# Four down groups by seven products in two of three parts of a decoder layer, with gate and up pairs on five banks

## The reference, cut to what matters

```python
x = x + jnp.concatenate([h_m, y_c], axis=-1) @ w_out      # after the mixer: h_m, y_c from a @ w_in
f = rmsnorm(x, g_ffn)
x = x + (jax.nn.silu(f @ w_gate) * (f @ w_up)) @ w_down   # (S,1024) @ (1024,2816) twice, (S,2816) @ (2816,1024)
e = rmsnorm(pe @ w_ple, g_ple)
x = x + jax.nn.sigmoid(x @ w_pg) * e
```

## Time and profile before

| | us |
|---|---|
| median of 3 runs | 2586.02 |
| lowest, highest | 2583.62, 2588.82 |
| profiled execution | 2582.85 |
| its span, first to last instruction | 2580.8 |

### The profile page before, as it was taken

How to read it: one execution, slowest core, us unless ns; L and a number is a source line. 1 busy time by engine, 2 the same in 40 slices (tenths; PEclk the granted TensorE clock), 3 DMA queues, 4 the chain that set the end, 5 groups by cost and what they waited for, 6 DMA issues and landing times.

```text
span 2580.8 us, 40956 instructions
## 1 busy us (share of the span) xinstructions
PE 2456.6 (95%) x15757; PEld 2395.0 (93%) x15757; DVE 1493.5 (58%) x2327; ACT 909.7 (35%) x1694; POOL 1010.7 (39%) x785
## 2 busy tenths in 40 slices
PE   7899888999999999999999999998999999999998
PEld 6888778999999989999999999998899999999997
DVE  7768987665555684477643333468357763333355
ACT  5344443343334443334312112355234422221133
POOL 5656755576666342122322122333222332322233
PEclk9999999999999999999999999999999999999999
DMA  7556644575666756575555544575667555565544
GB/s 230 211 181 239 219 152 173 202 264 215 212 228 218 229 159 205 182 259 162 180 163 196 203 138 165 180 231 181 192 188 255 169 196 158 189 219 167 175 133 149
DMA packets 285043, 501.00 MB, mean 194 GB/s; under 512 B 18427, under 2 KB 182612, under 8 KB 284342
## 3 DMA queue, kind: packets, MB, share of 16 engines
q1 hardware_dynamic: 212182, 273.59, 31.5%
q10 hardware_dynamic: 72672, 224.82, 26.6%
HBM read 374.70 MB, written 123.65 MB: 193 GB/s over the span
## 4 chain that ended last, share of the span: by engine, by line
PE 72%; DVE 7%; DMA 4%; issue 2%; ACT 1%; POOL 1%; DVEq 0%; SPq 0%; ACTq 0%; POOLq 0%
PE bank L612 23%; PE bank L614 22%; PE bank L613 22%; DMA wring<-weight_parts 2%; DVE qlo L1802 1%; POOL wring L2709 1%; DMA weight_parts<-wring 1%; DMA xs<-x_prompt 1%; DVE ess L2427 1%; PE bank L749 1%; PE bank L738 1%; PE bank L804 0%; PE bank L727 0%; DVE wraw L1792 0%; DVE hid L2444 0%
## 5 line engine op out<-in xcount | busy, mean ns | idle before, releaser
L2709 POOL TENSOR_TENSOR wring<-wraw,wring 128x512 fp32r<-128x512 f32 x525 | 766.6, 1468 | 1219.5 <-ACT wring L1288 1217.3
L612 PE MATMUL bank<-qhi,wring 128*128 128x352 f32 (+1 forms) x3540 | 1154.6, 326 | 69.9 <-DVE u L1913 13.9
L614 PE MATMUL bank<-qhi,wring 128*128 128x352 f32 (+1 forms) x3540 | 1137.2, 321 | 0.0
L613 PE MATMUL bank<-qlo,wring 128*128 128x352 f32 (+1 forms) x3540 | 1135.6, 321 | 0.0
L612 PEld LDWEIGHTS bank<-qhi,wring 128*128 128x128 f32 x3540 | 671.4, 190 | 95.7 <-issue 78.8
L613 PEld LDWEIGHTS bank<-qlo,wring 128*128 128x128 f32 x3540 | 670.7, 189 | 0.0
L614 PEld LDWEIGHTS bank<-qhi,wring 128*128 128x128 f32 x3540 | 668.8, 189 | 0.0
L1288 ACT ACTIVATE wring<-wraw 128x512 fp32r<-128x512 f32 x531 | 331.6, 629 | 712.1 <-PE bank L614 544.0
L612 PE MATMUL bank<-hid,wring 128*128 128x352 f32 (+1 forms) x1056 | 339.8, 322 | 12.2 <-DVE wide L2510 7.2
L614 PE MATMUL bank<-hid,wring 128*128 128x352 f32 (+1 forms) x1056 | 338.5, 321 | 0.0
L613 PE MATMUL bank<-hid,wring 128*128 128x352 f32 (+1 forms) x1056 | 337.7, 320 | 0.0
(11 more groups left out here) (322 smaller groups left out, 2405.2 us busy)
## 6 DMA issues: line engine op xcount, KB each, us to landing
wring<-weight_parts ACTq DMA_DIRECT2D x418, 512.0 KB, 4.5
weight_parts<-wring SPq DMA_DIRECT2D x201, 512.0 KB, 3.9
wraw<-w_down SPq DMA_DIRECT2D x33, 1024.0 KB, 7.2
wraw<-w_in SPq DMA_DIRECT2D x14, 1024.0 KB, 7.2
wraw<-w_gate SPq DMA_DIRECT2D x11, 1024.0 KB, 6.0
wraw<-w_up SPq DMA_DIRECT2D x11, 1024.0 KB, 6.2
wraw<-w_in SPq DMA_DIRECT2D x44, 256.0 KB, 5.1
wraw<-w_gate SPq DMA_DIRECT2D x44, 256.0 KB, 3.8
```

The costliest lines, as they stand in the source:

```text
L612: nc.tensor.matmul(o, hi, mh, start=begins, stop=False, skip_group_check=True)
L613: nc.tensor.matmul(o, hi, ml, start=False, stop=False, skip_group_check=True)
L614: return nc.tensor.matmul(o, lo, mh, start=False, stop=ends, skip_group_check=True)
L2709: nc.gpsimd.tensor_tensor(wlo[e % RING][:, :].rearrange(v, k=k), w.src, whi[e % RING][:, :].rearrange(v, k=k), ALU.subtract).then_inc(lo_d ...
```

## The change

It does five things.
1. In parts 1 and 2 the down groups g = 1 to 4 are done by seven products for each 512 columns of output (`down_by_sevens`): an entry holds a quarter of 2 k x 2 column blocks, and each product runs for two blocks m, on banks `DOWN_BANKS`. The hidden parts of the two pairs are the quarters B11, B12 and B2 of the activations; their differences T1 to T4 are made in `draw` by VectorE, and split into `dhi` and `dlo` by ScalarE and VectorE during the gate pair ahead of the down.
2. Part 0 makes and stores the sums of those down weights from its raw down weights: 32 more spares (`spares_of`, `DOWN_SPARES`), twelve in each group with pg's four: one after the down's last entry, three in the up pair, four in the next gate pair, four in the next up pair. A raw down weight keeps its buffer until its sums are made.
3. All gate and up pairs but up 1, gate 2 and up 2 have five banks and so the order `FIRST_PRODUCTS`.
4. Parts 1 and 2 have two raw buffers (the space of the other two holds `dlo` and `draw`); there SP loads raw r in step r. In part 0 from r = 26 on, SP first stores the parts of raw r-1 and then loads raw r+1.
5. Loads of pg's weights for the spares are issued at other steps, and the DMA scratch is 256 in place of 512.

```diff
-SPARE_PAIRS = {3: 0, 5: 4, 7: 8, 9: 12}
+DOWN_SEVEN = (1, 2, 3, 4)
+DOWN_SPARES = (3,), (1, 3, 5), (0, 2, 4, 6), (0, 2, 4, 6)
+PG_SPARE_LOADS = {24: 0, 32: 1, 38: 2, 44: 3}
+DOWN_PRODUCTS = PRODUCTS
+DOWN_BANKS = ((6, 7, 3, 4), (5, 2, 0, 1))
...
+        b = r % 2 if q else r % RAW_RING
...
-        if st == "gate":
-            return (0, 1, 2, 6, 7) if i == 0 else (0, 1, 2)
-        if st == "up":
-            return (3, 4, 5)
+        if st in ("gate", "up"):
+            own = (0, 1, 2) if st == "gate" else (3, 4, 5)
+            return own if (st, i) in (("up", 1), ("gate", 2), ("up", 2)) else own + (6, 7)
...
+    def spares_of(q, w, p):
+        g = (p - 1) // 2
+        if q or g not in DOWN_SEVEN:
+            return {}
+        of = [("down", g, 0)] * 4 + [("down", g, 1)] * 4 + [("pg", g - 1)] * 4
+        turn = {"down": 0, "up": 1 if p % 2 else 3, "gate": 2}[w]
+        before = sum(len(js) for js in DOWN_SPARES[:turn])
+        if w == "gate" and p % 2:
+            return {}
+        return {j: of[before + k] for k, j in enumerate(DOWN_SPARES[turn])}
...
+            def down_by_sevens(q, g):                                  # TensorE
+                begins = ("P1", "P6", "P5", "P7", "P4")
+                for a in range(2):
+                    for name in DOWN_PRODUCTS:
+                        e, op = n_entry[0], OPERAND_OF[name]
...
+                        entry_ready(e)
+                        if not a:
+                            pe.wait_ge(h_lo, down_operand_low(q.n, g, op))
+                        for m in range(2):
+                            first, second, third, fourth = DOWN_BANKS[m]
+                            bk = {"P1": first, "P2": first, "P5": second, "P3": second, "P6": third, "P4": third, "P7": fourth}[name]
+                            take(bk)
+                            for k in range(2):
+                                last = three(bank[bk][:, 0:q.N], hi[:, k, m, :], lo[:, k, m, :], dhi[:, op, k, 0:q.N],
+                                             down_low(op)[:, k, 0:q.N], name in begins and k == 0, k == 1)
...
-                    raw()                                              # SP
+                    now = q.n * RAWS + r
+                    if not q.n and r > 25:
+                        keep_parts((now - 1,))
+                    raws_to(now if q.n else r + 2 if r < 26 else r + 1)
...
+            def difference_high(q, p, name):                           # ScalarE
+                act.wait_ge(h_lo, HID_LOW[(q.n, p - 1, (0, "T1")) if name == "T1" else (q.n, p, (0, name))])
+                nc.scalar.activation(dhi[:, DIFFERENCES[name], :, 0:q.N], difference(name)[:, :, 0:q.N], ACT.Copy).then_inc(h_hi, 1)
...
-                    if s == 3 and p:
-                        act.wait_ge(h_lo, HIDDEN[(q.n, p - 1, 0, None)])
+                    if s in (1, 2) and p % 2 and seven_pair(q.n, p - 1):
+                        for name in (("T1", "T2"), ("T3", "T4"))[s - 1]:
+                            difference_high(q, p - 1, name)
+                    if p and s == (3 if p == 2 else 1):
+                        act.wait_ge(h_lo, HID_LOW[(q.n, p - 1, last_hidden(q.n, p - 1, 0))])
...
+            def hidden_parts(q, p, c):                                 # VectorE
+                if p % 2:
+                    nc.vector.tensor_tensor(dlo_first[:, c, 0:q.N], u[:, 0], dhi[:, 0, c, 0:q.N], sub).then_inc(h_lo, 1)
+                    nc.vector.tensor_tensor(t_1, u[:, 1], u[:, 0], sub).then_inc(h_lo, 1)
+                    return
+                nc.vector.tensor_tensor(dlo_rest[:, 0:2, c, 0:q.N], u, dhi[:, 1:3, c, 0:q.N], sub).then_inc(h_lo, 1)
+                nc.vector.tensor_tensor(t_2, u[:, 1], t_1, sub).then_inc(h_lo, 1)
+                nc.vector.tensor_tensor(t_3, u[:, 1], t_3, sub).then_inc(h_lo, 1)
+                nc.vector.tensor_tensor(t_4, u[:, 0], t_2, sub).then_inc(h_lo, 1)
...
+                    if s in (1, 2, 5, 6) and p % 2 and seven_pair(q.n, p - 1):
+                        difference_low(q, p - 1, {1: "T1", 2: "T2", 5: "T3", 6: "T4"}[s])
```

More of the change, by code:

```diff
@@ L1071, in raw, with raws_to @@
                     return
-                if r >= RAW_RING:
-                    sp.wait_ge(lo_done, raw_end[r - RAW_RING])
+                if raw_before[r] is not None:
+                    sp.wait_ge(lo_done, raw_end[raw_before[r]])
                 for where, src in raws[r]:
-                    sp.dma_start(wraw[r % RAW_RING][:, where].rearrange("p (k n) -> p k n", k=src.shape[1]), src)\
-                        .then_inc(landed[r % RAW_RING], 16)
+                    sp.dma_start(wraw[raw_buffer[r]][:, where].rearrange("p (k n) -> p k n", k=src.shape[1]), src)\
+                        .then_inc(landed[raw_buffer[r]], 16)
+            def raws_to(r):
+                while n_raw[0] <= r:
+                    raw()
             def keep_parts(which, names=None):
@@ L1239, in _ @@
                         keep_parts(pairs_[now - 1], lambda w: w.prepared >= raw_end[pairs_[now - 1][0]])
-                    if now and now not in pairs_ and now - 1 not in pairs_:
+                    if now and now not in pairs_ and now - 1 not in pairs_ and (q.n or r < 26):
                         keep_parts((now - 1,))
@@ L1283, in one_ahead @@
                 if w.first:
-                    act.wait_ge(landed[w.raw % RAW_RING], raw_landed[w.raw])
+                    act.wait_ge(landed[raw_buffer[w.raw]], raw_landed[w.raw])
                 if w.total:
@@ L1566, in e_square, with down_by_sevens @@
                 nc.scalar.activation(esq[:, :, 0:q.T], q.U[:, 2 * x:2 * x + 2, 0:q.T], ACT.Square).then_inc(e_sq, 1)
+            def down_by_sevens(q, g):
+                n = PAIR_NO[(q.n, "up", 2 * g + 1)]
+                for a in range(2):
+                    for name in DOWN_PRODUCTS:
+                        ahead()
+                        if name != "P1":
+                            continue
+                        for m in range(2):
+                            bk, key = DOWN_BANKS[m][0], (q.n, "down", g, 2 * a + m)
+                            act.wait_ge(*written[key + ("P1",)])
+                            act.wait_ge(*drained[(q.n, "down", g, m, "P7") if a else PAIR_KEYS[n - 2 + m] + ("P3",)])
+                            nc.scalar.activation(t1[(n + m) % 2][:, 0:q.N], bank[bk][:, 0:q.N], ACT.Copy).then_inc(free[bk], 1)
+                            t_used[n + m] = key + ("P7",)
             def late_silu(q, p):
@@ L1745, in link, with own @@
                 dve.wait_ge(dve_own, n_own[0])
+            def own(ins):
+                n_own[0] += 1
+                ins.then_inc(dve_own, 1)
+                return dve_own, n_own[0]
             def wait_buffer(t):
@@ L2858, in _ @@
                     if down_before(p) is not None:
-                        for k in range(8 if down_before(p) else 4):
+                        for k in range(14 if down_seven(q.n, down_before(p)) else 8 if down_before(p) else 4):
                             ahead()
```

242 lines of the change are left out of this document (180 added, 62 removed).

## The result

The changed kernel takes 2634.43 us (median; 2631.27 to 2638.08), the kernel before 2586.28 beside it: ratio 1.0184, 95% interval 1.017 to 1.0198. It is slower by 48.2 us. The forecast was 2593, in a range that ends at 2611: the sign came out, the size did not.

A forecast was written before the change was run, and what follows sets the result against it. TensorE was taken as the bound, busy 2456.6 of 2580.8 us. Terms -30.2 + 4 + 1 - 7.5 + 40 = +7.3 us gave 2590.2, and 3.2 more for the median gave 2593 us, range 2568 to 2611.

The forecast's parts named there:

- Products saved: Down groups of parts 1 and 2: 168 matmuls for 192 at an unchanged price each, -30.2 us.
- VectorE and ScalarE in parts 1 and 2: Gate pairs ahead of downs: ScalarE's wait delays a stored-weight load, 0.5 us in each of eight groups, +4 us.
- Five banks: Gate and up pairs: own banks for P7 and P4 remove part 0's 6.0 us bank waits; -7.5 us with weight waits.
- DMA and two raw buffers: Parts 1 and 2: more loads, raw weights issued only one pair ahead; late raws cost +1 us, bounds 0 and +3.
- The sums of part 0: Part 0's four groups: twelve sums where four were made, 10 us a group, +40 us; bounds +14.4 and +63.
- (a): Part 0's three pairs: ScalarE's cast waits for P5's ring slot, delaying the copy of t; 1.2 us each, 3.6 a group.
- (b): Part 0's gate and second up: cast waits for a store landing behind a raw load; 3.2 us twice, 6.4 a group.
- (c): Part 0's three pairs: GpSimd's 32 entries take 49.3 us, barely fitting beside the products; adds nothing more.
- The first two: Rivals on part 0's sums: stores land early, 2568 us (chance 0.27); stores land 1 us sooner, no change, 2585 us (0.16).
- the third: Rival: VectorE or the load behind ScalarE's wait bounds gate pairs before downs, parts 1 and 2; 2609 us, chance 0.09.
- The fourth: Rival: GpSimd and VectorE run serially in part 0's three pairs, 18 us a group, 2625 us; chance 0.06.
- The rule that stood with it: Two-input VectorE SBUF instructions and GpSimd SBUF reads share a port pair; the loser fully blocks, so all durations add up.

The follow-up runs named there:

- e11: Changed kernel with ScalarE's copies of differences spread over three steps and its wait moved behind a stored-weight load in parts 1 and 2: 2627.43 us.
- e5: Kernel before plus the five banks alone, P2 third: 2581.97 us, ratio 0.9980.
- e3: Changed kernel with both orders altered in part 0: SP stores ahead of the raw load, ScalarE's copy to t ahead of the casts: 2618.60 us.
- e9: e3 with VectorE's sums of the down weights cut to 32 of 512 columns, GpSimd's splits and transfers whole: 2599.13 us.
- e1: Changed kernel with only SP's order altered: in part 0 the first three part stores go ahead of the next raw load: 2620.91 us.
- e13: Changed kernel with both part 0 orders mended, ScalarE's wait moved, sums placed 2, 2, 4, 2, 2 and earlier raw loads: 2582.34 us.
- e15: Changed kernel with only e13's places of the sums and earlier raw loads, old orders kept: 2622.32 us.
- e10: e3 with GpSimd's splits of the down weights' sums cut to 32 of 512 columns, VectorE's sums and transfers whole: 2595.08 us.
- e16: e13 with one of the gate pair's two sums moved to the second up pair (2, 2, 4, 1, 3): 2609.89 us.
- e17: e13 with no sums in the gate pair and four in the second up pair (2, 2, 4, 0, 4): 2604.71 us.
- e2: Changed kernel with only ScalarE's order altered: in part 0 pairs with down sums, P1 is copied to t before the casts: 2621.41 us.

## Why the prediction was wrong, step by step

**Products saved, -30.2.** Right: four times 3.6 us in part 1 and 3.5 in part 2 are -28.4.

**VectorE and ScalarE in parts 1 and 2, +4.** The mechanism was right to the instruction: the load behind ScalarE's wait was expected at 6.5 us into the pair and went out at 6.6. It landed 5.8 us later (1561.2), not 4.5, near the case that the forecast priced at 1.2 us a group, and TensorE waited 0.85 us there. The price was some 5 to 8 us for the 4 forecast: e11, without that wait, is 7.9 us faster, and TensorE's waits on stored weights are 5.2 us less in its trace.

**Five banks, -7.5.** Right in its mechanism: the 6.0 us on the bank are gone. The gain is 4.3 us by e5, whose interval of 2.3 to 8.0 does not exclude 7.5; the waits that came instead, 2.3 us, stood in no term. **DMA and two raw buffers, +1**, was not measured by itself.

**The sums of part 0, +40.** This is the step that failed. The sums cost 73.2 us, 33 more than the forecast had, of an error of 41 in all (48.2 us measured against 7.3). With -28.4, +7.9 and -4.3 they add up to +48.4. Of the 33, some 14 are waits (54.0 us for the 40 of the forecast) and some 17 slow matmuls, of which the forecast has none. Term by term, for a group:
(a) was right: 1.2 us in the first up pair, as predicted.
(b) had the right chain and too small a price. A wait of 4.4 us (1.2 and 3.2) was forecast for the gate and for the second up pair; 5.8 and 5.6 were found, up to 8.2 in part 0. Two things make the difference: three casts in a row stand ahead of the copy of t (the forecast had two), and the first of them already waits 4.96 us for a landing. The kernel before has such a place in its trace: five stores issued from 614 to 621 us beside two raw loads took a median of 10.7 us, and ScalarE waited 6.29 us for a landing (until 627.32).
What was missing is the clock. Behind the two long waits of the group shown the granted clock was 0.50 for 19 and 14 matmuls, 4.6 us. The forecast took every matmul at 160 ns.
(c) "adds nothing" held for the changed kernel, whose waits name GpSimd nowhere in this stretch, but only because the copy of t was later still. e3 shows that with t in time GpSimd's line is the gate pair's bound at almost the same height (23.4 us for 22.4), which is why mending the orders gave 20 us and not 72.

The profile that was to come named the right wait, TensorE idle until the copy of t, with ScalarE waiting on stores; the group of part 0 was to take 90 to 100 us and took 102.60.

**The rivals.** The first two did not come about. Of the third, the load did land in about the 6 us that it asked for, but at a cost of some 8 us in all, not 20. The fourth, GpSimd and VectorE one after the other, had 18 us a group and 2625 us, nearest to the result, and yet not its cause: all 54.0 us of waiting were on ScalarE. It comes nearest to the bound that lies beneath, GpSimd's line in the gate pair. The rule that stood with it, from the Trainium skill (SBUF — State Buffer, "Who interferes with whom"), fits e3's gate pair better than the rows before: 1.73 us for a split and up to 1.79 for an addition, against medians of 1.30 and 0.684 elsewhere, is close to the sum that a full block would give, and e9's additions of 0.178 us that take 1.27 fit it too. In the pairs at large the engines still overlap: e3's three pairs take 51.9 us, not the 63.4 of the fourth rival (whose terms add up to 63.3).

**What decided between theories.** Order of the queues: shown as the cause in the second up pairs (e1 to e3 cure them). In the gate pairs the wait on t goes with the order mended, but the pairs get no shorter until the sums stand elsewhere too (e13 against e15). GpSimd's line: shown as the second bound of the gate pairs by e10. That VectorE makes its splits long is argued from their durations; that the added sums do it is not shown, as the splits of e9 stayed as long. A limit on the rate of the transfers is excluded by e10. The later theory that the gate pair goes with its number of sums fell with e16 and e17.

## What to carry to other kernels

Work that is put into an engine's idle time must also get in line: ask for each added store which transfer is issued just ahead of it, and for each added cast or sum what waits behind it in program order. When a wait is removed, look for the engine that is busy for nearly all of that stretch (here GpSimd, 21.6 of 23.4 us), because it takes over at once. And ask whether a stall of TensorE of some microseconds will have slow matmuls behind it; here they came to a third of the stall.

## What the hardware showed that was not expected

The granted clock of TensorE fell in the midst of a stage that runs at 1.00 throughout in the kernel before: after waits of 5.8 and 5.6 us, in which TensorE did nothing, the next 5.7 and 4.2 us ran at 0.50 (1.2 GHz), and then the clock came back. The length of the wait alone does not tell when: in e13 a wait of 2.9 us (until 548.88) has a stretch at 0.50 behind it, in e2 one of 3.0 (until 554.7) has none:

```profile
549.00:554.40 5.40, 5.40 (x19) 5.40 (x20) 4.21 (x5) 0.63 (x1) 3.03 (x3) 0.50 1.00 341
```

```profile
554.70:560.00 5.30, 5.30 (x33) 5.30 (x34) 5.27 (x7) 1.15 (x2) 4.01 (x3) 1.00 0.97 317
```

An addition of 128x32 elements on VectorE takes 0.178 us at the shortest and 1.27 at the median in e9's part 0, where GpSimd's splits run beside it; one of 128x512 has a median of 0.684 in the kernel before.

A store of 512 KB that lands in 2.7 us alone takes 7.5 us when it goes out 0.9 us behind a raw load of 1 MB, about as long as the load itself (7.2).
